# Mixers' opening in a two-block network: reciprocal ahead of a weight subtraction, four buffers for the normalised x, matmul waits by row block

## What is computed

```python
for l in range(DEPTH):                      # DEPTH = 2
    h = rms_norm(x, ffn1_norm[l])
    x = x + 0.5 * swiglu(h, ffn1_w_gate[l], ffn1_w_up[l], ffn1_w_down[l])
    h = rms_norm(x, mix_norm[l])            # x * rsqrt(mean(x*x) + 1e-6) * w
    (nq, nkc, nvc, nks, nvs, nkw, nvw, ngate, sq, sk, sv, wq, wk, wv, bgate) = jnp.split(
        h @ w_in[l], SPLIT_POINTS, axis=-1)
    ...                                     # three attentions, gates, w_out
    h = rms_norm(x, ffn2_norm[l])
    x = x + 0.5 * swiglu(h, ffn2_w_gate[l], ffn2_w_up[l], ffn2_w_down[l])
```

## Time and profile before

| | us |
|---|---|
| median of 3 runs | 2693.69 |
| lowest and highest | 2693.33 to 2693.91 |
| the profiled execution | 2689.35 |
| its span | 2687.5 |
| TensorE busy (share of the span) | 2510.4 (93%) |
| VectorE busy | 1658.9 (62%) |
| ScalarE busy | 1179.8 (44%) |
| GpSimd busy | 428.5 (16%) |

### The profile page before, as it was taken

One profiled execution on the slowest core, in us unless ns is written; L12 is line 12 of the kernel. 1 busy time (PEld: TensorE's weight loads), 2 busy tenths in 40 slices (PEclk: granted clock), 3 DMA queues, 4 the chain that ended last, 5 costly groups with the idle time before them and its releaser, 6 DMA issues.

```text
span 2687.5 us, 41648 instructions
## 1 busy us (share of the span) xinstructions
PE 2510.4 (93%) x17737; PEld 2290.9 (85%) x17737; DVE 1658.9 (62%) x2442; ACT 1179.8 (44%) x1900; POOL 428.5 (16%) x387
## 2 busy tenths in 40 slices
PE   8998979999999898899998988899999899998998
PEld 7998868999999896789997765688888799998998
DVE  4786646688887764667776776553342654555653
ACT  5444545544444355555544543342232444344552
POOL 1311015432023000452410120100001011011000
PEclk8999979999999999999999998999999999999999
DMA  7667454576776756346775120132232333334452
GB/s 227 207 225 191 126 159 113 163 229 229 228 235 217 233 130 196 94 127 235 251 269 169 48 75 0 49 109 95 93 108 91 109 94 110 99 106 142 151 194 95
DMA packets 398126, 404.56 MB, mean 151 GB/s; under 512 B 58743, under 2 KB 382611, under 8 KB 397684
## 3 DMA queue, kind: packets, MB, share of 16 engines
q1 hardware_dynamic: 395192, 394.14, 46.8%
q10 hardware_dynamic: 2748, 7.76, 0.8%
HBM read 397.67 MB, written 4.19 MB: 150 GB/s over the span
## 4 chain that ended last, share of the span: by engine, by line
PE 70%; DVE 19%; ACT 6%; issue 2%; DMA 2%; POOL 1%; ACTq 0%; DVEq 0%; SPq 0%; POOLq 0%
PE bank L657 21%; PE bank L659 20%; PE bank L658 20%; DVE rounded L2145 6%; PE bank L665 3%; ACT rounded L1463 3%; DVE plain L2134 2%; PE bank L1402 2%; PE bank L670 1%; DMA plain<-in_w_in 1%; DVE rounded L2191 1%; DVE plain L2366 1%; DVE plain L2155 1%; POOL plain L3067 1%; PE bank L1011 1%
## 5 line engine op out<-in xcount | busy, mean ns | idle before, releaser
L657 PE MATMUL bank<-rounded 128*128 128x256 f32 (+1 forms) x3784 | 1155.5, 305 | 60.3 <-DVE rounded L2191 26.4
L658 PE MATMUL bank<-rounded 128*128 128x256 f32 (+1 forms) x3784 | 1134.6, 300 | 0.0
L659 PE MATMUL bank<-rounded 128*128 128x256 f32 (+1 forms) x3784 | 1133.4, 300 | 0.0
L2145 DVE TENSOR_TENSOR rounded<-plain,rounded 128x1024 fp32r<-128x1024 f32 (+2 forms) x578 | 677.1, 1218 | 508.8 <-ACT rounded L1463 508.5
L657 PEld LDWEIGHTS bank<-rounded 128*128 128x128 f32 x3784 | 734.9, 194 | 110.9 <-DVE rounded L2191 33.9
L1463 ACT ACTIVATE rounded<-plain 128x1024 fp32r<-128x1024 f32 (+2 forms) x634 | 621.9, 1034 | 346.1 <-PE bank L659 284.6
L659 PEld LDWEIGHTS bank<-rounded 128*128 128x128 f32 x3784 | 735.0, 194 | 20.3
L658 PEld LDWEIGHTS bank<-rounded 128*128 128x128 f32 x3784 | 735.7, 194 | 19.3
L657 PE MATMUL bank<-rounded,rounded 128*128 128x256 f32 (+1 forms) x1376 | 421.0, 306 | 30.1 <-DVE rounded L2145 22.7
L658 PE MATMUL bank<-rounded,rounded 128*128 128x256 f32 (+1 forms) x1376 | 417.6, 304 | 0.0
L659 PE MATMUL bank<-rounded,rounded 128*128 128x256 f32 (+1 forms) x1376 | 417.5, 303 | 0.0
(11 more groups left out here) (266 smaller groups left out, 2013.8 us busy)
## 6 DMA issues: line engine op xcount, KB each, us to landing
plain<-in_mlp_w SPq DMA_DIRECT2D x64, 1024.0 KB, 5.2
plain<-in_ada_w SPq DMA_DIRECT2D x48, 1024.0 KB, 5.5
plain<-in_ffn_w_gate SPq DMA_DIRECT2D x44, 1024.0 KB, 5.5
plain<-in_ffn_w_up SPq DMA_DIRECT2D x44, 1024.0 KB, 5.6
plain<-in_ffn_w_down SPq DMA_DIRECT2D x32, 1024.0 KB, 5.1
plain<-in_w_in SPq DMA_DIRECT2D x32, 1024.0 KB, 5.4
plain<-in_od_w_in SPq DMA_DIRECT2D x32, 1024.0 KB, 5.5
plain<-in_ffn_w_down SPq DMA_DIRECT2D x16, 768.0 KB, 5.8
```

The costliest lines, as they stand in the source:

```text
L657: pe.matmul(dst, a[0], b[0], start=first and i == 0, stop=False)
L658: pe.matmul(dst, a[0], b[1], start=False, stop=False)
L659: ins = pe.matmul(dst, a[1], b[0], start=False, stop=last and i == n - 1)
L2145: dve.tensor_tensor(low, raw, top, SUB).then_inc(*done(("lo", m, half)))
```

## The change

VectorE: the reciprocal is taken before the weights of `sv` are subtracted. The normalised x gets four buffers, the two of the products and the two of the squares, which are free by then (`b.four`). VectorE makes the products of blocks 0 to 3, then subtracts `sv`'s weights, then goes on in pairs: subtract block c (even), products of c+4 and c+5. ScalarE rounds, and GpSimd subtracts the odd blocks, out of the same four buffers. TensorE runs `flush_one` ahead of block 3 instead of block 4, and the wait for all eight blocks is gone: `values` waits for block k ahead of its products. `values` is called for `wv` and `nv` too, where these waits have been made already and vanish. `normed` without a shift isn't used any more.

```diff
--- before.py
+++ after.py
@@ -291,6 +291,7 @@
         b.rstd = self.take(n)
         b.sq = [self.take(n), self.take(n)]
         b.tmp = [self.take(n), self.take(n)]
+        b.four = b.tmp + b.sq
         b.acc = b.tmp[0]
         return b
 
@@ -812,8 +813,11 @@
             b = bank(s, name)
             ready(m)
             for tile in range(2):
-                ins = product(b[:, tile * 256:tile * 256 + 256],
-                              [(hx(k, tile * 128, tile * 128 + 128), part(m, k, 0, 256)) for k in range(8)])
+                for k in range(8):
+                    for x in new(at("h", s, k)):
+                        pe.wait_ge(*x)
+                    ins = product(b[:, tile * 256:tile * 256 + 256],
+                                  [(hx(k, tile * 128, tile * 128 + 128), part(m, k, 0, 256))], k == 0, k == 7)
             ins.then_inc(*done((s, name), ("unit", m)))
 
         def headsum(name, n):
@@ -869,14 +873,11 @@
             for k in range(8):
                 for y in new(at("early", s, k)):
                     pe.wait_ge(*y)
-                if x == 0 and k == 4:
+                if x == 0 and k == 3:
                     flush_one(was)
                 for e, m in enumerate((m0, m1)):
                     ins = product(bs[e][:, x * 256:x * 256 + 256], [(part(m, k, x * 128), hx(k, 256, 512))], k == 0, k == 7)
         ins.then_inc(*done((s, "sqk"), ("unit", m0), ("unit", m1)))
-        for k in range(8):
-            for y in new(at("h", s, k)):
-                pe.wait_ge(*y)
         values(U[s, "sv"], "sv")
         for jj in range(2):
             m = U[s, "nq", jj]
@@ -1494,20 +1495,15 @@
         act.activation(HSr[:, 0, c, 256:512], X[:, c, 0:256], ACT.Copy, scale=col("mix_norm", l * 8 + c)).then_inc(
             *done(("earlyhi", s, c)))
 
-    def normed(s, n, shift=None):
+    def normed(s, n, shift):
         tmp = (M.two if n == 512 or s[0] in "po" else M.one).tmp
         for c in range(8):
             for q in range(n // 256):
                 ss = slice(256 * q, 256 * q + 256)
-                if shift is None:
-                    for x in new(at(s, "tmp", c)):
-                        act.wait_ge(*x)
-                    act.activation(HSr[:, 0, c, 0:n], tmp[c % 2][:, 0:n], ACT.Copy, scale=1.0).then_inc(*done(("hx", s, c, 0)))
-                else:
-                    for x in new(at(s, "tmp", c, q)):
-                        act.wait_ge(*x)
-                    act.activation(HSr[:, 0, c, ss], tmp[c % 2][:, ss], ACT.Identity, bias=shift(c, q), scale=1.0).then_inc(
-                        *done(("hx", s, c, q)))
+                for x in new(at(s, "tmp", c, q)):
+                    act.wait_ge(*x)
+                act.activation(HSr[:, 0, c, ss], tmp[c % 2][:, ss], ACT.Identity, bias=shift(c, q), scale=1.0).then_inc(
+                    *done(("hx", s, c, q)))
 
     def setup():
         for dst, src in M.rows[0]:
@@ -1634,7 +1630,10 @@
             act.wait_ge(*x)
         hi(U[s, "sq"] + 2)
         root(was, M.one.rstd)
-        normed(s, 256)
+        for c in range(8):
+            for x in new(at(s, "tmp", c)):
+                act.wait_ge(*x)
+            act.activation(HSr[:, 0, c, 0:256], M.one.four[c % 4], ACT.Copy, scale=1.0).then_inc(*done(("hx", s, c)))
 
         def headsq(name, src, n, free=None):
 
@@ -2168,7 +2167,7 @@
         dve.scalar_tensor_tensor(HSr[:, 1, c, 256:512], X[:, c, 0:256], col("mix_norm", l * 8 + c), HSf[:, 0, c, 256:512],
                                  MUL, SUB).then_inc(*done(("early", s, c)))
 
-    def normed(s, was, n, weight, shift=None):
+    def normed(s, was, n, weight, shift):
         sc = M.two if n == 512 or s[0] in "po" else M.one
         for c in range(8):
             tmp = sc.tmp[c % 2]
@@ -2178,18 +2177,12 @@
                     dve.wait_ge(*x)
                 dve.scalar_tensor_tensor(tmp[:, ss], X[:, c, ss], weight(c, q), sc.rstd[:, ss], MUL, MUL).then_inc(
                     *done((s, "tmp", c), (s, "tmp", c, q)))
-            if shift is None:
-                if c % 2 == 0:
-                    for x in new(at("hx", s, c, 0)):
-                        dve.wait_ge(*x)
-                    dve.tensor_tensor(HSr[:, 1, c, 0:n], tmp[:, 0:n], HSf[:, 0, c, 0:n], SUB).then_inc(*done(("h", s, c)))
-            else:
-                for q in range(n // 256):
-                    ss = slice(256 * q, 256 * q + 256)
-                    for x in new(at("hx", s, c, q)):
-                        dve.wait_ge(*x)
-                    dve.scalar_tensor_tensor(HSr[:, 1, c, ss], tmp[:, ss], shift(c, q), HSf[:, 0, c, ss], ADD, SUB).then_inc(
-                        *done(("h", s, c)))
+            for q in range(n // 256):
+                ss = slice(256 * q, 256 * q + 256)
+                for x in new(at("hx", s, c, q)):
+                    dve.wait_ge(*x)
+                dve.scalar_tensor_tensor(HSr[:, 1, c, ss], tmp[:, ss], shift(c, q), HSf[:, 0, c, ss], ADD, SUB).then_inc(
+                    *done(("h", s, c)))
         here(s, "begun", "dve")
 
     def residual(s, key, name, o, l, which, seqs, *out):
@@ -2370,9 +2363,24 @@
         stage(was)
         for x in new(*[at("flat", i) for i in range(8, 12)]):
             dve.wait_ge(*x)
+        root(was, M.one.rstd)
+
+        def times(c):
+            for x in new(at(was, "rstd"), at("h", s, c - 4) if c >= 4 else None):
+                dve.wait_ge(*x)
+            dve.scalar_tensor_tensor(M.one.four[c % 4], X[:, c, 0:256], col("mix_norm", l * 8 + c), M.one.rstd, MUL,
+                                     MUL).then_inc(*done((s, "tmp", c)))
+
+        for c in range(4):
+            times(c)
         lo(U[s, "sq"] + 2)
-        root(was, M.one.rstd)
-        normed(s, was, 256, lambda c, q: col("mix_norm", l * 8 + c))
+        for c in range(0, 8, 2):
+            for x in new(at("hx", s, c)):
+                dve.wait_ge(*x)
+            dve.tensor_tensor(HSr[:, 1, c, 0:256], M.one.four[c % 4], HSf[:, 0, c, 0:256], SUB).then_inc(*done(("h", s, c)))
+            if c < 4:
+                times(c + 4)
+                times(c + 5)
 
         def exact(key, r, m, tmp, name=None):
 
@@ -3079,9 +3087,9 @@
         b_ = M.mix
         stage(was)
         for c in range(1, 8, 2):
-            for x in new(at("hx", s, c, 0)):
+            for x in new(at("hx", s, c)):
                 pool.wait_ge(*x)
-            pool.tensor_tensor(M.HSr[:, 1, c, 0:256], M.one.tmp[1][:, 0:256], M.HSf[:, 0, c, 0:256], SUB).then_inc(
+            pool.tensor_tensor(M.HSr[:, 1, c, 0:256], M.one.four[c % 4], M.HSf[:, 0, c, 0:256], SUB).then_inc(
                 *done(("h", s, c)))
         for blk in range(1, 12):
             lo(U[s, "bg", blk] + 3)
```

## The result

The changed kernel takes 2681.48 us in the median of 5 runs (2677.40 to 2683.27), the one before beside it 2693.33 (2692.24 to 2693.91): a ratio of 0.9955, 95% interval 0.9941 to 0.9970, or 11.9 us less. The forecast was 2684.4 us, in a range from 2680.3 to 2688.3. The profiled execution took 2681.13 us against 2689.35.

What follows compares the result with a forecast made beforehand. TensorE, busy 93% of the span, bounds the kernel; gains of 4.2 us (5.6 - 1.4) and 5.1 us (6.5 - 1.4), together 9.3, off the 2693.69 us median give 2684.4 us, range 2680.3 to 2688.3.

Steps and rivals of the forecast that it cites:

- The openings: Starts of the two mixers, where TensorE waits for normalised x, then runs at low clock: at most 5.6 and 6.5 us.
- rival 2: In the openings, the remaining waits still send TensorE to 1.2 GHz: 5.4 us gained, 2688.3 us; chance 0.12.
- the waits by block: TensorE's sv products wait for each block separately; called the part that pays, leaving 1.4 us of waiting in the first opening.
- Rival 4: TensorE's first sv product still starts only when block 7 is there: 0.1 us per mixer, 2693.5 us; chance 0.04.
- rival 3: Later load traffic, not its start, fixes the mixer's end: up to all the gain lost, 2693.7 us; chance 0.06.
- rival 5: GpSimd's four subtractions stretch beside a busy VectorE: slower by 3.7 us a mixer, 2701 us; chance 0.04.
- turns: In the openings, GpSimd and two-input VectorE operations alternate: weights ready at 248.35, block 4 subtracted by 251.8 us.
- 1.4 us of waits: TensorE in the first opening's sv products: 0.23 us for block 2, 1.18 for block 4, 0.02 for block 7.
- VectorE's idle time: First opening, ahead of the reciprocal: VectorE idles from 238.71 us until the root lets it start at 241.19.
- the reciprocal's 1.07 us: VectorE in the first opening: reciprocal ahead of the weights' subtraction starts at 241.19 instead of 242.26, 1.07 us earlier.
- The clock's reason: TensorE in the openings: no wait over 1.2 us, so clock stays up; 1.00 after 1.8 us, 0.54 after 2.7.
- its own 1.2 us: The longest TensorE wait expected in an opening's sv products, 1.18 us for VectorE's subtraction of block 4.

Runs made afterwards that it cites:

- the runs made once more: The changed kernel, unaltered, run again beside the kernel before on the same chip: 2678.34 us in the median against 2689.58, ratio 0.9951.
- the kernels in which TensorE doesn't wait: Changed kernel with sv's weights subtracted ahead of the reciprocal, 2676.37 us; changed kernel with all block subtractions on VectorE, 2677.92 us.
- the last kernel tried: Changed kernel with sv's weights subtracted ahead of the reciprocal and TensorE's one wait for all eight blocks put back: 2682.34 us, before 2687.72.

## Why the prediction was right, and where not

**Right: what bounds and what pays.** The openings could give 5.6 and 6.5 us; without any wait of TensorE they gave 5.6 and 6.6. That TensorE's products start one pitch behind `sk`'s, that no clock falls (rival 2) and that the waits by block are the part that pays is borne out: alone they bring 9.0 us, the order and the buffers alone 2.9. The Trainium skill, "TensorE: Matmul & The Clock Gate", HAM oscillation, tells of a kernel in which TensorE waited some 3 to 5 us for a DMA at every K-tile and was at the low clock again each time. The changed kernel's waits were one of some 0.6 us in each opening, with a granted clock of 1.00 behind it, so this case doesn't test that. Rival 4 is out by the start of `sv`'s products, rival 3 (later transfers) by the whole time: its median is 11.9 us lower, and 11.2 us in the runs made once more; rival 5's long GpSimd subtraction did come, 3.37 us, but nothing hung on it.

**The step that was mis-sized: turns.** The prediction let GpSimd in between product 4 and the weights and again between their halves, and so had the weights ready at 248.35, block 4 at 251.8 and 1.4 us of waits. Measured, less the 2.29 us: weights at 247.03, block 4 at 251.12 (where VectorE's next subtraction starts), a loss of 0.8 us an opening (17.85 less the 17.03 of the kernels in which TensorE doesn't wait). Of it 0.71 us stand ahead of block 4's first product (253.54 less 252.71 is 0.83, against a pitch of 0.12; the list of waits has 0.56 of it). VectorE kept GpSimd out over both halves of the weights and block 0's subtraction, where I had let it in twice. 0.6 us an opening, 1.2 in all: 10.5 instead of 9.3. The rest to 11.9 lies within what the runs scatter.

**The step that was missed: VectorE's idle time.** The prediction books the reciprocal's 1.07 us (0.96 measured) as gained and writes the idle time ahead of it down without a price. It has one: the weights' 2.36 us fitted there, and moved behind the products they delay block 0 and all that follow. With the weights first the change would have gained 1.6 us more; with two buffers the new order costs 1.1 us an opening. Of the three parts the waits by block give 9.0, four buffers 3.1 on top, and the order takes 1.6 back. This split holds for parts added in this order only: with the weights first and four buffers but the one wait, 8.25 us were gained, and the waits by block would add 3.9.

**The clock's reason was weaker than it looked.** The prediction kept the clock up because it was still at 1.00 after a wait of 1.8 us and at 0.54 after one of 2.7. The 2.7 us wait was followed by 1.00 in the changed kernel, and a wait of 1.72 us by 0.57 in the trace of the last kernel tried. The forecast of the clock held with waits of 0.6 us; its own 1.2 us didn't come about, and in the openings waits of 1.0 and 1.7 us went well too.

**The profile and the median.** I had carried the gain from one execution to the median. The medians moved by 11.9 us, the profiled executions by 8.2, the openings by 10.5: the profiled executions had moved 2.3 us the wrong way before the change had acted. Only the lengths could show its size; that the median came so near the forecast is in part luck.

## What to carry to other kernels

Where an engine waits for a group of blocks and then needs them one by one, put the waits at the blocks: here that alone gave 9.0 of the 10.5 us, and no wait was then long enough for the clock to fall in an opening. Ask of an instruction moved ahead what it will idle for, and leave work there that fits. And compare a local stretch with two ends that the change doesn't touch when the whole time scatters by as much as the gain.

## What the runs showed of the hardware

GpSimd didn't get between VectorE's two-input instructions as long as these followed one another without a pause: one subtraction took 3.37 us where 0.74 is usual, and 0.74 again when VectorE was made to wait first. The Trainium skill, "GPSIMD Engine Reference", Specifications, names the shared SBUF interfaces and the contention. That it can be this one-sided no row before had shown. The earlier trace rows had turns, and ScalarE's roundings of the two halves tell what was different there:

```profile
480.02 1.99 ACT L1463 ACTIVATE rounded<-plain 128x1024 fp32r<-128x1024 f32 x2
```

GpSimd asked at 481.78, and the rounding that VectorE's second half needs ended at 482.01. So that half wasn't ready yet when GpSimd asked, and GpSimd came first. In the changed kernel all of VectorE's three subtractions were ready before GpSimd asked at 246.88: the weights were rounded by 243.09 and block 0 by 246.32. Whether a pause of VectorE decides, or which instruction was ready first, no run parts: both fit all traces here.

TensorE's clock in the openings stayed at 2.4 GHz over single waits of 0.6, 1.0 and 1.7 us and over two of 0.95 us close together, and fell to 1.2 GHz after 2.9 and 3.0 us. But the length of a wait doesn't decide it alone. Here is one wait of 2.40 us, at the same place of the same kernel, in the two traces of the change (the 3 us behind it; granted clock behind the count):

```profile
1377.22:1380.22 3.00, 3.00 (x26) 1.00 0.67 203
...
1374.22:1377.22 3.00, 3.00 (x18) 0.67 0.61 196
```

In the twelve traces of this case that wait was followed by 1.00 four times and by 0.57 to 0.70 eight times. All 174 waits of 2.9 us or more ahead of which the clock was up had 0.74 or less in the 3 us behind them; of 231 such waits between 0.7 and 1.5 us one had less than 0.9 (0.78 after 1.27 us); between 1.5 and 2.8 us both happened. So one trace with a clock that stayed up over 1.7 us, or fell after 2.7, says little about the next.
